# Scan of a hybrid diffusion step: mask and decay rows in one product per half bank, factor exponentials ahead of the weights, and four fold buffers in the first norm

## The reference

```python
def adaln_params(cond, w, b):
    return jnp.split(jax.nn.silu(cond) @ w + b, N_MOD, axis=-1)

def modulate(x, g, shift, scale):
    return rmsnorm(x, g) * (1 + scale[:, None, :]) + shift[:, None, :]
```

```python
cum = jnp.cumsum(dtc * A, axis=1)
seg = jnp.where(causal, cum[:, :, None] - cum[:, None], -jnp.inf)
wts = jnp.einsum('bign,bjgn->bijg', Cc, Bc)[..., None] * jnp.exp(seg) * dtc[:, None]
y = jnp.einsum('bijgr,bjgrp->bigrp', wts, xc)
y = y + jnp.einsum('bign,bgrpn->bigrp', Cc, h) * jnp.exp(cum)[..., None]
w_end = jnp.exp(cum[:, -1:] - cum) * dtc
h = h * jnp.exp(cum[:, -1])[..., None, None] + jnp.einsum('bjgn,bjgr,bjgrp->bgrpn', Bc, w_end, xc)
```

## Time and profile before

| | |
|---|---|
| median of 3 runs | 3533.86 us (3529.67 to 3542.34) |
| profiled execution, its own time | 3524.27 us |
| its span, first to last instruction | 3522.5 us |
| mean granted TensorE clock | 0.963 of full |
| first norm block | starts at 10 us, next block's first product at 81.72 us |
| scan block | 776 us to 993 us |

### The profile page before, as it was taken

How to read it: one execution, slowest core, us unless ns; L and a number is a source line. 1 busy time by engine, 2 the same in 40 slices (tenths; PEclk the granted TensorE clock), 3 DMA queues, 4 the chain that set the end, 5 groups by cost and what they waited for, 6 DMA issues and landing times. The chain is left out here.

```text
span 3522.5 us, 47527 instructions
## 1 busy us (share of the span) xinstructions
PE 3330.8 (95%) x18392; PEld 2905.6 (82%) x18392; DVE 1956.0 (56%) x3348; ACT 996.0 (28%) x2021; POOL 541.3 (15%) x551
## 2 busy tenths in 40 slices
PE   7999999998979899999999889999979999999997
PEld 5665665655568899999999878888879999999996
DVE  4995551336767644555445577654455554455546
ACT  2212542434445322112211143322243112211221
POOL 1010100003434211001110002332232011100110
PEclk6999999999989999999999999999989999999998
DMA  5661111133154211111111212222242111111111
GB/s 231 241 263 46 37 51 40 44 83 102 44 197 119 66 40 48 42 42 36 48 42 42 71 36 70 66 66 60 72 128 59 43 37 48 43 45 39 40 48 54
DMA packets 188027, 257.92 MB, mean 73 GB/s; under 512 B 18112, under 2 KB 164040, under 8 KB 182080
## 3 DMA queue, kind: packets, MB, share of 16 engines
q1 hardware_dynamic: 187876, 255.86, 22.1%
HBM read 231.67 MB, written 24.15 MB: 73 GB/s over the span
## 5 line engine op out<-in xcount | busy, mean ns | idle before, releaser
L1867 PE MATMUL PS<-AHL,WH 128*128 128x384 f32 x3072 | 782.7, 335 | 6.0 <-DVE WL L2216 6.0
L1867 PE MATMUL PS<-Y,WH 128*128 128x384 f32 x3072 | 780.0, 334 | 3.1 <-issue 3.1
L2236 DVE SCALAR_TENSOR_TENSOR XT<-PS,MOD,XT 128x384 f32<-128x384 f32 (+2 forms) x1024 | 495.4, 514 | 224.5 <-PE PS L1867 224.2
L1867 PEld LDWEIGHTS PS<-AHL,WH 128*128 128x128 f32 x3072 | 557.2, 189 | 6.6 <-DVE WL L2216 6.6
L1867 PEld LDWEIGHTS PS<-Y,WH 128*128 128x128 f32 x3072 | 554.4, 188 | 4.2 <-issue 3.7
L1867 PE MATMUL PS<-AHL,WL 128*128 128x384 f32 x1536 | 514.7, 335 | 0.0
L1867 PE MATMUL PS<-Y,WL 128*128 128x384 f32 x1536 | 513.1, 334 | 0.0
L2223 DVE TENSOR_TENSOR AHL<-SQ,AHL 128x384 fp32r<-128x384 f32 x192 | 157.2, 819 | 430.3 <-ACT AHL L1972 430.3
L2150 POOL TENSOR_TENSOR SQ<-RT 128x384 f32<-128x384 f32 x192 | 179.8, 937 | 1319.6 <-ACT RT L1967 1300.2
L1961 ACT ACTIVATE WH<-WU 128x1024 fp32r<-128x1024 f32 x128 | 135.5, 1059 | 730.0 <-DMA WU<-in_wff 730.0
L624 PE MATMUL PS<-HT,WR 128*128 128x384 f32 x960 | 324.5, 495 | 12.0 <-PEq L532 7.4
(11 more groups left out here) (361 smaller groups left out, 4480.0 us busy)
## 6 DMA issues: line engine op xcount, KB each, us to landing
WU<-in_wff SPq DMA_DIRECT2D x128, 512.0 KB, 3.6
XT<-in_wmod SPq DMA_DIRECT2D x13, 2048.0 KB, 10.5
F<-in_wmod SPq DMA_DIRECT2D x9, 2048.0 KB, 9.1
OWR<-in_wslots SPq DMA_DIRECT2D x24, 768.0 KB, 5.1
WR<-in_wslots SPq DMA_DIRECT2D x8, 2048.0 KB, 8.2
PW<-in_wslots SPq DMA_DIRECT2D x24, 512.0 KB, 4.5
OWOR<-in_wslots SPq DMA_DIRECT2D x24, 512.0 KB, 4.2
EB<-cum_rows SPq DMA_DIRECT2D x36, 256.0 KB, 4.3
```

Source lines behind the costliest of these rows:

```text
L1867: mm = nc.tensor.matmul(out, wt(w), x, start=(n == 0 and i == 0), stop=(n == len(terms) - 1 and i == 2))
L2236: ins = nc.vector.scalar_tensor_tensor(out=x, in0=PS[:, 3 + j % 4, a - c * TC:e - c * TC], scalar=MOD[:, l, 40 + b, cond:cond + 1], in1=x, ...
```

## The change

- The exponents of a bank are made by two products of 256 columns, each alone in its half of the bank, in place of two accumulating products of 512. For a half f the stationary operand pick_r[d, f] holds the strict triangle in the 64 partitions of that half and a row of ones in two partitions of the other half. The moving operand CR[b] holds -1e30 on the diagonal in the one and the decay rows (high, low) in the other, so one product gives the mask and the decay.
- CR becomes four buffers, one for each b, with 2 rows for each half. So rows_in issues 8 transfers a step in place of 1, each pair behind the exponents of the step before that used the same buffer. cum_parts is laid out for it, by 32 stores in place of 4.
- The constants for it are written by ACT in the convolution block (16 instructions at i == 10) in place of 4 at the start of the scan block.
- ACT exponentiates the factors of a step ahead of its weights (inter(n), then weights(n)); before, inter(n) came behind weights(n).
- ACT reads a head's exponents from PSUM in two pieces of 64.
- In the first norm the first four slots have a fold buffer each. Slots 2 and 3 are folded over six blocks in place of four. RB lies in F1, all eight blocks of x are scaled by DVE, and POOL has nothing to do. ACT modulates blocks 0, 2, 4, 6 in place of 0, 1, 5, 6.

```diff
-        CR = at_word("cum_r", 36864, [P, SH * P], F32R)
+        CR = [at_word(f"cum_r{n}", 36864 + 512 * n, [P, 2, 4, 64], F32R) for n in range(4)]
+        pick_r = at_word("pick_r", 38912, [P, 2, 2, P], F32R)
...
-            if n >= 2:
+            if n >= 4:
                 act.wait_ge(mod_used.sem, n - 1)
...
-            folded = 4
-            pool_blocks, act_blocks = (5, 6, 7), (0, 1, 5, 6)
+            folded = (4, 4, 6, 6)
+            act_blocks = (0, 2, 4, 6)
...
-                        if k not in pool_blocks:
-                            dve.wait_ge(x_in[min(k // 3, 2)].sem, 16)
-                            scale(nc.vector, k).then_inc(scaled_ready.sem, 1)
+                        dve.wait_ge(x_in[min(k // 3, 2)].sem, 16)
+                        nc.vector.tensor_tensor(xk[:, k, :], xk[:, k, :], RB, ALU.mult).then_inc(scaled_ready.sem, 1)
...
                     for part, rows in enumerate((rows_hi, rows_lo)):
-                        sp.dma_start(cum_parts[d, :, part, :, :].rearrange("t h i -> h t i"),
-                                     rows[r, :].bitcast(F32).rearrange("h (t i) -> h t i", t=NT)).then_inc(rows_stored.sem, 16)
+                        for b in range(4):
+                            for f in range(2):
+                                src = rows[32 * d + 4 * b:32 * d + 4 * b + 4, :].bitcast(F32).rearrange("h (t f i) -> h t f i", t=NT, f=2)
+                                sp.dma_start(cum_parts[d, :, b, f, part, :, :].rearrange("t h i -> h t i"), src[:, :, f, :])\
+                                  .then_inc(rows_stored.sem, 16)
...
+                    if i == 10:
+                        act.wait_ge(rows_stored.sem, rows_stored.at(34 * 16))
+                        for n in range(4):
+                            act.activation(CR[n][:, :, :, :], ident.rearrange("p (f i) -> p f i", f=2).unsqueeze(2).broadcast_to((P, 2, 4, 64)),
+                                           ACT.Copy, scale=NEG).then_inc(act_own.sem, act_own.one())
...
                 def rows_in(n):
-                    if n >= 2:
-                        sp.wait_ge(exponents_made.sem, exponents_made.at(4 * (n - 1)))
-                    r = 64 * (n % 2)
-                    sp.dma_start(CR[r:r + 2, :].bitcast(F32), cum_parts[n % 2, n // 2, :, :, :].rearrange("s h i -> s (h i)"))\
-                      .then_inc(rows_spread[n % 2].sem, 16)
+                    for b in range(4):
+                        if n >= 1:
+                            sp.wait_ge(exponents_made.sem, exponents_made.at(4 * (n - 1) + b + 1))
+                        for f in range(2):
+                            r = slice(64 - 64 * f, 66 - 64 * f)
+                            sp.dma_start(CR[b][r, f, :, :].bitcast(F32), cum_parts[n % 2, n // 2, b, f, :, :, :]).then_inc(rows_spread[b].sem, 16)
...
-                    nc.tensor.matmul(PS[:, 2 + j % 2, :].rearrange("p (h i) -> p h i", h=4), ident_r[:, :],
-                                     mask_r[:, n % 2, :].unsqueeze(1).broadcast_to((P, 4, P)), start=True, stop=False)
-                    nc.tensor.matmul(PS[:, 2 + j % 2, :], ones_r[r, :], CR[r, 512 * b:512 * b + 512], start=False, stop=True)\
-                      .then_inc(exponents_made.sem, 1)
+                    pe.wait_ge(rows_spread[b].sem, rows_spread[b].at(32 * (n + 1)))
+                    for f in range(2):
+                        mm = nc.tensor.matmul(PS[:, 2 + j % 2, 256 * f:256 * f + 256], pick_r[:, n % 2, f, :],
+                                              CR[b][:, f, :, :].rearrange("p h i -> p (h i)"), start=True, stop=True)
+                    mm.then_inc(exponents_made.sem, 1)
...
                 weights(0)
                 inter(0)
+                inter(1)
                 weights(1)
-                for n in range(NS):
-                    if n + 1 < NS:
-                        inter(n + 1)
-                    if n + 2 < NS:
-                        weights(n + 2)
+                for n in range(2, NS):
+                    inter(n)
+                    weights(n)
```

75 lines of the change are left out of this document (31 added, 44 removed).

## The result

The changed kernel takes **3484.5 us** (median, 3482.6 to 3488.9) beside 3535.2 for the kernel before in the same measurement: ratio 0.9857, 95% interval 0.9837 to 0.9877. The forecast was 3515, with a range down to 3500; the gain is 50.7 us and not 18.7. Two later executions of the kernel before (4243 and 3941 us) were in a slower state, the first at a granted clock of 0.731, and count in no median or ratio here.

What follows compares the result with a forecast made beforehand. It took PE to bound the first norm's end and a loop of PE and DVE the scan. Gains of 6.2 (norm), 11.1 (scan pairs) and 1.4 (scan start), 18.7 us in sum, took 3533.86 to 3515; range 3500 to 3526.

Steps and rivals of the forecast that it cites:

- The price of a bank: In the scan, a bank's products cost 0.43 us in place of 0.86, so a pair goes from 20.72 to 18.1 us.
- The clock: In the scan, seven of eight pairs hold a low stretch costing 3.15 us each; gain 11.1 us, ends 8 and 33.
- The base: Whole kernel: the profiled execution, 3524.3, lies 9.6 us under the median; the same difference set against 3533.86 gives 3515.
- the clock stays up more often: Rival for the scan: at most four clock drops in eight pairs, gain 28 to 41 us, 3493 to 3506; chance 0.17.
- The first norm: First norm: the gains start at 67.9 to 68.8 in place of 74.39, behind DVE's scalings; taken as 6.2 us gained.
- The convolution block: Convolution block: SP's small stores and ACT's 16 new instructions taken as 0, with 0 to +5 us as bounds.
- Factors ahead of the weights: Scan: at most 0.24 us a step to gain at L1635; taken as 0, with up to 4 us as a bound.
- The scan's start: Ahead of the first zero-row product, two banks save 0.72 us each, gain 1.4; small transfers may add up to 2.5.
- DVE level with PE: Scan's odd step: DVE at 7.99 us and PE at 8.09 are level, so nothing more comes from PE alone.

Runs made afterwards that it cites:

- e13: Kernel before, with the second product of each bank made with 128 rows (126 of zeros) in place of two: 3508.3 us, ratio 0.9932.
- e10: Changed kernel plus one 128-row product of 512 columns ahead of the two of each bank, values overwritten: 3501.4 us, ratio 0.9913.
- e14: e13 with the second product reading two rows again, nothing else changed: 3530.4 us, ratio 0.9994.
- e1: Kernel before, unchanged, profiled and timed again: 3533.4 us, ratio 1.0001.
- e5: Changed kernel with the two 256-column products of each bank issued twice: 3504.2 us, ratio 0.9920.
- e6: Changed kernel plus a one-row product of 512 columns ahead of the two of each bank: 3511.1 us, ratio 0.9937.
- e9: e5 with the extra pair of products made from two rows in place of 128: 3513.2 us, ratio 0.9952.
- e2: Kernel before with the first norm's part of the change alone: 3527.4 us, ratio 0.9981.
- e3: Kernel before with everything of the change except the first norm's part: 3484.2 us, ratio 0.9868.
- e4: Kernel before with ACT's factors ahead of the weights, nothing else: 3534.7 us, ratio 1.0005.
- e12: Changed kernel with ACT's order of before, factors behind the weights: 3488.8 us, ratio 0.9878.
- e15: Changed kernel, unchanged, profiled and timed again: 3484.4 us, ratio 0.9862.
- e8: Changed kernel with the second and third yl loads issued behind the decay rows of step 2: 3479.9 us, ratio 0.9850.
- e7: Kernel before with the two-row second product of each bank made with 64 rows, 62 of zeros: 3528.2 us, ratio 0.9984.
- e11: Kernel before with the mask product issued twice in one bank of each step: 3541.5 us, ratio 1.0029.
- e16: e8 with the zero products made from 128 rows of zeros in place of one: 3496.3 us, ratio 0.9900.

## Why the prediction was wrong

The steps that failed are three: the price of a bank, the cost and number of low stretches, and the base that the gain was taken from. The last two carry most of the miss.

**The price of a bank.** The prediction took one product of 512 columns at 0.43 us from the earlier trace rows and so a bank at 0.86, then halved it by columns. But 0.43 is no price of columns. e13 has the same 1024 columns in 0.55 us, and e10 shows 0.31 for a first product of 512 and 0.24 for 512 more in two pieces. What the rows of before showed was a two-row product between products of 128 rows: with two rows in place of 128 the second product starts 0.09 us later and what follows it 0.19 later still (e14 and e13). The Trainium skill, TensorEngine Tiling (Array Packing), Key Properties, says that changing the tiling mode drains the engine. If a product of 2 or 64 rows counts as another mode, it pays on both sides, and the times of e14 and e13 agree with that (0.28 a bank); no run shows the drain itself. The prediction did not weigh it. The bank came to 0.32 behind a read, the pair to 17.62 where 18.1 was forecast: 0.5 a pair, 4 us of the miss. The bounds of a bank, 0.43 to 0.86, were wrong at the lower end.

**The clock: the largest part of the miss.** Forecast were seven low stretches of 3.15 us cost, 22 us; there were three of 1.57, 4.7 us, which is 17.3 us. The reasoning was that a longer wait brings more of them, each at its old price. Both halves failed. The wait grew as forecast, to 1.62 and 0.40 us, and fewer came: the kernel before has seven with 1.23 us of waiting (e1), the changed one three or two with 2.02. In e5, e10 and e13 pairs with 1.8 us of waiting do have one nearly every time, so the wait is not without a part, but it does not set the number. And they are 3.4 us long and not 6.8. What changes the length is a product of few rows in every bank: with it 6.8 us and more (e1, e6, e9, e14), without it 3.4 (e5, e10, e13, but for one of 6.8 in each of the last two), at the same or more columns. That the rows do it is shown; whether by the time that they add to a pair (20.2 to 20.7 against 19.0 to 19.1) or otherwise is not. Why the pair of 17.62 us has a low stretch in two or three cases of eight only stays open, too. The rule of the Trainium skill that the prediction cited (TensorE: Matmul & The Clock Gate, HAM oscillation), a return to the lower clock in each turn, fits e14 (eight of eight) and nearly e5 (seven), but not the changed kernel (three).

**The base.** The difference was worked out on an execution with four low stretches and then set against the median. The usual scan of before has seven or eight, 189.6 us in e1 against 178.3. The 9.6 us by which that execution lay under the median were in the very stretch that the change removes; they belonged to the gain. Against the median of the final measurement this is 10.9 us of the miss. Another 4.4 are the profiled execution of after lying above its own median.

So the 32 us of the miss are: 4.2 and 17.3 for the pair and the clock, 15.3 for the base, 0.9 for the norm, 4.3 for the clock's course up to the scan block, less 5.6 at the scan's start (a loss of 4.2 for a gain of 1.4) and 4.5 behind the scan.

**The rival that came true** is "the clock stays up more often", to which I gave 0.17 and 28 to 41 us. On the profiled executions the gain was 35.3, within it; against the medians it lay beyond its end, by the base.

**The first norm** was right: gains at 67.28 behind DVE's scalings (67.9 to 68.8 was said), no fold over 1 us, the next block 7.1 us earlier for 6.2; alone it is worth 6.7 us (e2), though it can't be told on top of the rest (e3). That the fold of 3098 ns was POOL's hold fits the profile without POOL, where none is over 0.95 us.

**The convolution block** cost nothing, as taken; a small store took SP 0.36 us, not the 0.6 of the nearest row.

**Factors ahead of the weights**: nothing, as taken (e4, e12).

**The scan's start** was taken as a gain of 1.4 and was a loss of 4.2 in this profile and of 0.6 between e1 and e15; the gain is in neither. That small transfers ahead of the yl loads "may add up to 2.5" was named and not counted. The rows of step 1 now make PE wait as well (5.41 us), and those of step 2, behind the yl loads in both kernels, arrive later. e8 shows that the order of these loads holds the start: 25.2 us to the first zero-row product, of which the first pair takes half back.

**DVE level with PE** was right: PE's two waits and DVE's 1.68 us of idle say that both bound the pair.

Of the 46 us that the scan part is worth, the rows alone give 22 (e13 against e14). The other 24 (e13 to e3, across two measurements) come with half the columns: 1.37 us a pair, 11 us, and 10 us of low clock (two low pairs against seven); the rest lies outside of the eight pairs. e5 is the straight test of this half: it issues the same products twice in the changed kernel, changes nothing else, and stands 20 us above it. That leaves some 4 us, no more than two measurements differ by, for what no run takes apart from the columns: ACT's reading in two pieces and the eight row transfers a step.

## What to carry to other kernels

Price a matmul from a row only if what stands around it has the same number of rows; a product with a handful of rows among full ones took 0.2 to 0.28 us more here, and padding it with zeros to 128 rows took that away. Where a loop shows low stretches of the clock in some of its turns, take the base from several executions and price the case with all of them too. And before an edit moves one engine by tenths of a microsecond, look at what POOL is doing when DVE's critical operation starts: an order that was lucky can turn, and a wait helps only on the POOL operation that does the holding.

## What the runs showed of the hardware

- A product with 1, 2 or 64 rows between products of 128 rows takes 0.2 to 0.28 us more than the same with 128 rows (e6 and e10, e9 and e5, e14 and e13; the 64 rows of e7 left the pair at 20.77).
- With such a product in each bank, eight a pair, low stretches are 6.8 us and longer, without them mostly 3.4; the four one-row zero products of a pair are in all of these runs. In e11, with one full product more a step and the two-row product kept, they are 13.7 and 6.8 in turn.
- An addition of two SBUF operands on DVE (128x1024, float32) takes 1.23 us alone. When it starts while POOL runs an operation of its own it ends 1.08 us behind that one: 1.41, 1.57, 1.77 or 2.88 us, as 0.33, 0.48, 0.7 or 1.80 us of POOL's are left (e15, before, e15, e16). POOL's takes 1.90, and 2.88 behind DVE's. The Trainium skill, SBUF — State Buffer, SBUF: two separate sides, says that the first to start holds the shared port pair for its whole instruction; the traces agree.
- The same program can show low clock in four or in seven of the eight pairs (the profile of before, and e1), 11 us apart.
- Low stretches do not follow the length of PE's wait: three low pairs of eight with 1.0 us of waiting (e9), seven with 1.8 (e13), two with 2.02 (e15).
